# Order of the small steps between two tiles of an input projection: squares, first query copy, rotation

## The reference

```python
h = rms_norm(x, attn_norm)                       # x * rsqrt(mean(x*x) + eps) * g
splits = np.cumsum(IN_SIZES)[:-1].tolist()
q_lat, kv_lat, kr_raw, qb_raw, kb_raw, vb_raw, iq_raw, ik_raw, iw = jnp.split(h @ w_in, splits, axis=-1)
qa = (rms_norm(q_lat, q_a_norm) @ w_q_b).reshape(b, l, N_HEADS_A, NOPE_DIM + ROPE_DIM)
qa_nope, qa_rope = qa[..., :NOPE_DIM], rope(qa[..., NOPE_DIM:], pos)
c_kv = rms_norm(kv_lat, kv_a_norm)
k_rope = rope(kr_raw, pos)
qB = partial_rope(qb_raw.reshape(b, l, N_HEADS_B, HEAD_DIM_B), pos, ROT_DIM_B)
# kB, iq, ik: partial_rope likewise; vB and iw stay as they are
```

## Time and profile before

| what | value |
|---|---|
| median of 3 runs | 4259.19 us (4246.77 to 4260.42) |
| the profiled execution's own time | 4255.5 us |
| its span, first to last instruction | 4253.4 us |
| PE busy | 3778.7 us, 89% |
| DVE, ACT, POOL busy | 52%, 40%, 33% |
| `project`'s loop: first and last `xt_hi` | 15.2 and 535.9 us |

### The profile page before, as it was taken

The page is one execution under the profiler, slowest core; times in us unless marked ns, Lnnn a source line. Parts: engine busy times, 40 slices in busy tenths (PEclk is TensorE's granted clock), DMA queues, the critical chain, the costliest instruction groups (busy, mean ns, idle before and its releaser), DMA issues. The chain is left out here.

```text
span 4253.4 us, 59485 instructions
## 1 busy us (share of the span) xinstructions
PE 3778.7 (89%) x20612; PEld 2900.5 (68%) x20612; DVE 2200.5 (52%) x4236; ACT 1702.1 (40%) x3219; POOL 1386.8 (33%) x890
## 2 busy tenths in 40 slices
PE   7999976877888888888895699899999999999998
PEld 5777743556655555666663577688788778889986
DVE  4222223699988888889953533343044134304421
ACT  3333322556656666666561222232233233223311
POOL 0000000556555565455001000244444444444332
PEclk9999988689989999999996599999999999999999
DMA  4222222110100000000002165334343433433331
GB/s 169 73 80 86 77 65 58 42 34 26 30 22 20 17 20 10 17 16 15 12 6 48 35 229 200 128 89 151 97 118 89 153 114 97 145 106 99 89 109 56
DMA packets 337092, 324.13 MB, mean 76 GB/s; under 512 B 53088, under 2 KB 272832, under 8 KB 336896
## 3 DMA queue, kind: packets, MB, share of 16 engines
q1 hardware_dynamic: 323040, 271.35, 21.9%
q10 hardware_dynamic: 7344, 26.74, 1.5%
q0 software_dynamic: 6528, 23.73, 1.5%
HBM read 251.57 MB, written 71.43 MB: 76 GB/s over the span
## 5 line engine op out<-in xcount | busy, mean ns | idle before, releaser
L2193 DVE TENSOR_SCALAR_CACHE_REDUCE at_hit<-at_score,at_su 128x384 bf16<-128x384 f32 (+13 forms) x406 | 599.6, 1477 | 5.3
L1639 DVE TENSOR_TENSOR ff_a_lo<-ff_prod,ff_a_hi 128x512 f32 (+1 forms) x110 | 410.8, 3735 | 170.7 <-ACT ff_a_hi L1591 170.7
L1494 POOL TENSOR_TENSOR fh_w_lo<-fh_stage,fh_w_hi 128x2048 fp32r<-128x2048 f32 x67 | 309.2, 4615 | 463.4 <-ACT fh_w_hi L1577 463.4
L1925 PE MATMUL at_p_t<-at_ident,at_prob 128*128 128x128 f32 x2176 | 333.6, 290 | 131.8 <-ACT at_prob L2005 130.6
L1494 POOL TENSOR_TENSOR ff_w_lo<-fh_stage,ff_w_hi 128x2048 fp32r<-128x2048 f32 (+1 forms) x68 | 296.3, 4357 | 432.0 <-ACT ff_w_hi L1577 412.8
L1925 PEld LDWEIGHTS at_p_t<-at_ident,at_prob 128*128 128x128 f32 x2176 | 250.7, 145 | 210.9 <-ACT at_prob L2005 177.5
L2005 ACT ACTIVATE at_prob<-at_prob,at_st 128x1024 f32<-128x1024 f32 (+7 forms) x384 | 342.9, 897 | 123.3 <-DVE at_st L2162 123.0
L2020 ACT ACTIVATE at_probt<-at_p_t 128x512 f32<-128x512 f32 (+3 forms) x640 | 313.5, 533 | 163.8 <-PE at_p_t L1925 161.2
L2102 POOL TENSOR_TENSOR at_rel<-at_rel,at_iws 128x512 f32<-128x512 f32 (+3 forms) x304 | 283.7, 933 | 174.7 <-ACT at_rel L2027 174.0
L95 PE MATMUL ff_bank<-fh_h_hi,fh_w_hi 128*128 128x512 f32 (+1 forms) x880 | 309.8, 352 | 10.5 <-DVEq L1626 6.8
L1587 ACT ACTIVATE ff_prod<-ff_bank 128x512 f32<-128x512 f32 (+1 forms) x110 | 57.0, 518 | 646.0 <-PE ff_bank L97 645.8
(11 more groups left out here) (288 smaller groups left out, 8477.9 us busy)
## 6 DMA issues: line engine op xcount, KB each, us to landing
fh_stage<-in_w_gate SPq DMA_DIRECT2D x86, 512.0 KB, 4.0
fh_stage<-in_w_up SPq DMA_DIRECT2D x86, 512.0 KB, 5.2
fh_stage<-in_w_down SPq DMA_DIRECT2D x40, 1024.0 KB, 5.2
pj_xt<-in_xT SPq DMA_DIRECT2D x17, 512.0 KB, 3.6
pj_x<-in_x SPq DMA_DIRECT2D x17, 512.0 KB, 4.4
mx_o<-scr_o SPq DMA_DIRECT2D x17, 512.0 KB, 7.1
mx_x<-in_x SPq DMA_DIRECT2D x17, 512.0 KB, 3.6
scr_x<-mx_x ACTq DMA_DIRECT2D x17, 512.0 KB, 8.2
```

Of the source, the lines that this page charges most:

```text
L1494: pool.tensor_tensor(w_lo[a][:, 0:w], stage[a][:, 0:w], w_hi[a][:, 0:w].bitcast(F32), ALU.subtract).then_inc(s_wlo, 1)
L1639: dve.tensor_tensor(a_lo[:, ds(2 * q + a, 1), to], prod[b][:, 0:gr.Nh].unsqueeze(1), a_hi[:, ds(2 * q + a, 1), to].bitcast(F32), ALU.subtr ...
L1925: mm = pe.transpose(p_t[t_turn.at(n, f) % 2][:, b * P:(b + 1) * P], prob[h % 2][:, a + b * P:a + (b + 1) * P], ident[:, :])
L2193: step(dve.tensor_scalar(h_, s_, cand.bitcast(F32), 0.0, ALU.is_ge, ALU.add, cnt))
```

## The change

ACT: `split` is divided into `cut` (`xt_hi`) and `power` (squares of `x`). In the loop, `power(i + 1)` stands between the copies of z chunks 1 and 2 of tile i; it no longer waits for the four z copies. The copy of QA0 stands ahead of the wait for DVE's inverse means and their root. `cut(i + 1)` follows, then the copies QA1 to T1, and last the root of the next row. DVE: `split` is divided into `cut` (`xt_lo`) and `mean`. `mean(i + 1)` opens the body, with a wait for ACT's root of the row before, since it rewrites that root's input; the rotation stands ahead of `cut(i + 1)`. Nothing changes on PE and SP, nor for the last tile.

```diff
--- before.py
+++ after.py
@@ -238,22 +238,23 @@
             act.sem_inc(s_ev, NB)
             for n in range(6):
                 act.sem_inc(s_qst[n], 16)
-            def split(i):
+            def cut(i):
                 act.wait_ge(s_xt, 16 * i + 16)
                 if not (isinstance(i, int) and i == 0):
                     act.wait_ge(s_zmm, 4 * i)
                 act.activation(xt_hi[:, :, :], xt[:, :, :], ACT.Copy).then_inc(s_hi, 1)
+
+            def power(i):
                 act.wait_ge(s_x, 16 * i + 16)
                 if not (isinstance(i, int) and i == 0):
                     act.wait_ge(s_sq, i)
-                    act.wait_ge(s_zev, 4 * i)
                 act.activation(squares[:, :], x[:, :], ACT.Square, accum_out=stat[:, 0:1]).then_inc(s_sq, 1)
 
             def rstd(i):
                 act.wait_ge(s_inv, i + 1)
                 act.activation(stat[:, 2:3], stat[:, 1:2], ACT.Sqrt).then_inc(s_rstd, 1)
 
-            def take_z(i):
+            def take_z(i, steady=False):
                 act.wait_ge(s_rstd, i + 1)
                 if not (isinstance(i, int) and i == 0):
                     act.wait_ge(s_zr, i)
@@ -262,12 +263,16 @@
                 for c, (a, b) in enumerate(CH):
                     if c == len(CH) - 1 and not (isinstance(i, int) and i == 0):
                         take_fill(i - 1, B_QL)
+                    if c == 2 and steady:
+                        power(i + 1)
                     act.wait_ge(s_zmm, 4 * i + c + 1)
                     act.activation(z[:, a:b], zp[c][:, 0:b - a], ACT.Copy, scale=stat[:, 2:3]).then_inc(s_zev, 1)
                 act.wait_ge(s_zev, 4 * i + 4)
                 act.activation(squares_z[:, 0:QL], z[:, C_Q:C_Q + QL], ACT.Square, accum_out=stat[:, 4:5]).then_inc(s_zsq, 1)
                 act.wait_ge(s_zsq, 2 * i + 1)
                 act.activation(squares_z[:, 0:KVL], z[:, C_KV:C_KV + KVL], ACT.Square, accum_out=stat[:, 5:6]).then_inc(s_zsq, 1)
+                if steady:
+                    take_fill(i - 1, B_QA0)
                 act.wait_ge(s_zinv, i + 1)
                 act.activation(stat[:, 8:10], stat[:, 6:8], ACT.Sqrt).then_inc(s_zrs, 1)
 
@@ -289,28 +294,30 @@
                     act.wait_ge(s_qr, i + 1)
                 act.activation(out, src, ACT.Copy).then_inc(s_ev, 1)
 
-            def post(i):
-                for b in range(B_QA0, NB):
+            def post(i, b0):
+                for b in range(b0, NB):
                     take_fill(i, b)
 
-            split(0)
+            cut(0)
+            power(0)
             for k in range(KD):
                 act.wait_ge(s_wg, k + 1)
                 act.activation(w_hi[:, k, :], stage[k % S][:, :], ACT.Copy).then_inc(s_whi, 1)
             rstd(0)
             take_z(0)
-            split(1)
+            cut(1)
+            power(1)
             rstd(1)
             act.wait_ge(s_wlo, KD)
             with act.Fori(1, LAST) as i:
-                take_z(i)
-                split(i + 1)
+                take_z(i, steady=True)
+                cut(i + 1)
+                post(i - 1, B_QA1)
                 rstd(i + 1)
-                post(i - 1)
             take_z(LAST)
-            post(LAST - 1)
+            post(LAST - 1, B_QA0)
             take_fill(LAST, B_QL)
-            post(LAST)
+            post(LAST, B_QA0)
 
         @block.tensor
         def _(pe):
@@ -385,9 +392,13 @@
             dve.sem_inc(s_qr, 1)
             own = Count(dve, s_vec, 0)
 
-            def split(i):
+            def cut(i):
                 dve.wait_ge(s_hi, i + 1)
                 dve.tensor_tensor(xt_lo[:, :, :], xt[:, :, :], xt_hi[:, :, :].bitcast(F32), ALU.subtract).then_inc(s_lo, 1)
+
+            def mean(i):
+                if not (isinstance(i, int) and i == 0):
+                    dve.wait_ge(s_rstd, i)
                 dve.wait_ge(s_sq, i + 1)
                 own.done(dve.tensor_scalar(stat[:, 3:4], stat[:, 0:1], 1.0 / D, EPS, ALU.mult, ALU.add))
                 dve.reciprocal(stat[:, 1:2], stat[:, 3:4]).then_inc(s_inv, 1)
@@ -446,7 +457,8 @@
                        cos, sin, [tmq[:, a, :, :] for a in range(4)], (s_qr, i + 2))
 
             own.round(0)
-            split(0)
+            cut(0)
+            mean(0)
             dve.wait_ge(s_gain, 16)
 
             def gain(k):
@@ -462,15 +474,18 @@
                 dve.tensor_tensor(w_lo[:, k, :], stage[k % S][:, :], w_hi[:, k, :].bitcast(F32), ALU.subtract).then_inc(s_wlo, 1)
             dve.wait_ge(s_const, 16 * N_CONST)
             z_means(0)
-            split(1)
+            cut(1)
+            mean(1)
             z_rows(0)
             n0, own.per = own.n, own.n + 5
 
             def body(i, last=False):
+                if not last:
+                    mean(i + 1)
                 z_means(i)
+                rotate_qa(i - 1)
                 if not last:
-                    split(i + 1)
-                rotate_qa(i - 1)
+                    cut(i + 1)
                 z_rows(i)
 
             with dve.Fori(1, LAST) as i:
```

## The result

The changed kernel takes 4220.38 us (median of 5 runs, 4217.4 to 4228.85), the one before 4257.01 in the runs beside it: ratio of the means 0.9921, 95% interval 0.9904 to 0.9938, thus 33.6 us less, between 26 and 41 (the medians differ by 36.6). The forecast was 4230, in a range of 4217 to 4247, and a gain of 28.8 us. The profiled execution has a span of 4215.3 us.

The account below looks back on a forecast made before the run. TensorE bounds the kernel, through idle time in each turn's tail and clock dips. 16.8 us (15 turns x 1.12) plus 12.0 (8 dips x 1.50) made 28.8: span 4253.4 to 4224.6, forecast 4230 as median, range 4217 to 4247.

Parts of the forecast that it names:

- The squares cost nothing between the chunks: On ACT, squares needing about 1.14 us fit the 4.89 us idle ahead of the chunk-2 copy, if x has landed.
- c0: PE's first product of the next tile, counted from q (L347 rows' start): from q+9.13 to q+8.01, 16.8 us in 15 turns.
- Rival E: Slower: ACT's new wait for x delays the chunk-2 copy and the copies behind it; time 4272, chance 0.03.
- The 4.3 us more: Slack on ACT after the chunk-2 and QL copies before PE needs QL; x's landing would have to exceed 9.3 us.
- They, and the root behind them, were what PE waited for: Squares and root held ACT 1.79 us ahead of the copies PE needs; moving them brings IQ0 1.82 us earlier.
- the two gaps: On the way to c0: rotation to low half on DVE, taken as 0.28 us; low half to c0, 0.15.
- The dips: PE's clock at 1.2 GHz after the tail's idle in 8 of 15 turns; all gone, 8 x 1.50 = 12.0 us.
- Rivals B and C: PE's dips stay: B, once in two turns, time 4242, chance 0.13; C, in every turn, time 4253, chance 0.04.
- Rival D: Another wait holds QB0's copy on ACT, so IQ0 stays near q+7; time 4259, chance 0.04.
- The swap: DVE rotates before making the low half; worth about nothing alone, perhaps slightly against, c0 near q+7.9 without it.
- QA0 ahead of the root: On ACT, QA0's copy takes the 0.61 us hole before L272; it fits, as two copies took 0.87.

Follow-up runs that it names:

- e1: Changed kernel with the squares back in the tail, behind the high half and ahead of QA1's copy; ratio to the kernel before 0.9962.
- e6: Only the change's first part (squares, mean, root moved); QA0 next to QA1 behind the high half, low half ahead of the rotation; ratio to the kernel before 0.9933.
- e4: Kernel before with DVE's new order alone (mean, rotation, low half), ACT as before; ratio to the kernel before 1.0007.
- e7: Changed kernel with two useless 128x1024 copies on ACT between the copies of QA1 and QB0; one execution, 4247.85 us.
- e5: Changed kernel with the next input's low half made by POOL in the loop, DVE only rotating and writing rows; ratio to the kernel before 0.9985.
- e10: Changed kernel with the low half on POOL and ACT writing the queries' unrotated part straight from PSUM, without DVE's copy; ratio to the kernel before 0.9956.
- e8: Changed kernel with one useless 128x1024 copy on ACT between the copies of QA1 and QB0; one execution, 4215.79 us.
- e3: Changed kernel with DVE's old order, low half ahead of the rotation; ratio to the kernel before 0.9921.
- e2: Changed kernel with QA0's copy back behind the high half, next to QA1; ratio to the kernel before 0.9925.

## Why the prediction was right

- *The squares cost nothing between the chunks:* shown by the idle time behind them, 1.04 us in the turn above and never under 0.64. The forecast had 0.6 there. It let DVE's row copy start at c0+0.13 and x be issued at c0+10.9; the row copy starts at c0-0.32 (238.97), before the low half has ended, and x is issued at c0+10.46. Rival E didn't come about, as no load was late enough to hold chunk 2. The 4.3 us more that it reckoned before PE would stall stay an estimate: no run has a later load.
- *They, and the root behind them, were what PE waited for:* IQ0 was forecast at q+5.15 and came at q+5.23; e1 gives the squares' share, e6 shows that this part alone is enough, and the root's share, 0.75 us, is read from rows. The 0.08 by which IQ0 is later lies in QB0's copy, which starts at q+4.59 where the last turn has q+4.51, both times behind a copy of QA1 at q+4.07; why isn't shown.
- *c0:* forecast q+7.68 to q+8.10, taken as 8.01, measured 7.85. Of the two gaps the first was 0.04 and not 0.28: the wait of the earlier trace rows stands ahead of `z_rows`, which has three waits of its own, and doesn't go over to a neighbour with one (that this is the reason is argued, not shown). The second was 0.24, not 0.15. So this term was 15 x 1.25 = 18.8 us in place of 16.8. The idle time in front of c0 was to be 0.5 to 0.8 us and is 0.36 in PE's row: c0 is 0.61 later than the q+7.24 that T0 alone would allow, but T0's rows are drawn until q+7.49.
- *The dips:* forecast 12.0 us back, measured 8 x (33.15 - 31.63) = 12.2. Rivals B and C fall: both short gaps are there and the granted clock is 1.00 over all 15 turns. The Trainium skill's rule that the prediction cited against itself ("TensorE: Matmul & The Clock Gate", section "A second HAM failure mode: psum-queue depth-cycling") tells of a clock that swings because of short idle times; this trace doesn't bear it out for the 0.33 and 0.36 us left here. What the kernels with dips have in common:

  | kernel | longest idle time, us | idle times of the tail, sum | c0 at full clock | dipped turns of 15 |
  |---|---|---|---|---|
  | e4 | 1.97 | 2.52 | q+9.65 | 8 |
  | before | 2.07 | 2.26 | q+9.13 | 8 |
  | e7 | 2.22 | 2.22 | q+8.89 | 6 |
  | e5 | 1.57 | 1.90 | q+8.77 | 4 |
  | e1 | 0.93 | 1.57 | q+8.68 | 0 |
  | e10 | 1.23 | 1.56 | q+8.43 | 0 |
  | e8 | 1.13 | 1.13 | q+7.85 | 0 |
  | changed | 0.36 | 0.69 | q+7.85 | 0 |

  My theory in e7 was the length of the wait in one piece. All waits with dips are longer than all without, but the count doesn't follow it: 2.22 us gave fewer dips than 1.97. It does follow the sum of the tail's idle times, and the place of c0. No run separates these, so which of them counts stays open. One reading of the prediction was loose: its two windows in the earlier trace rows start at q+8.33 and q+7.11, not at the same place; at q+8.33 the short turn (250.52 to 253.82) is granted 1.00 as well, so nothing hangs on it.
- *Rival D* fell: IQ0 moved by 1.74 us, so nothing else held QB0's copy near its old place.
- *The swap:* said to be worth about nothing or slightly against; it is against, by 0.25 us a turn (e3). The remark had the size a little low: it put c0 near q+7.9 without the swap, and it is at q+7.63.
- *QA0 ahead of the root:* my step counted it as fitting its hole, which it does; it buys nothing (e2).

Sum by measured terms: 18.8 + 12.2 = 31.0 us, where the forecast had 28.8. The time's 33.6 agrees with 31 within its interval; the rest of the span's 38.1 lies in stages that the change doesn't touch. The terms were low by 2.0 and 0.2 us. Luck had a part in the second: that all dips would go came true, but what keeps them away isn't shown.

## What to carry to other kernels

Ask of each instruction in front of a copy that frees a PSUM bank whether TensorE waits for it; what belongs to the next tile can go where its engine waits for products anyway, even if it then waits for a load there, as long as some of that idle time is left behind it. The turn without the next tile's work, at a loop's end, is a free model of the loop with that work moved. And price an idle time twice: with waits of 2.07 and 0.19 us cut to 0.33 and 0.36, the turn at full clock got 1.25 us shorter, and the dips that went with them had cost 0.8 us a turn more on the mean.

## What was not expected of the hardware

In two places GpSimd held up VectorE in full, not by a share, and as far as rows show it was not slowed itself: its subtraction took 2.36 us, and `at_qb_lo`, of the same shape and on the same engine in the kernel before, 2.36 on the mean. While GpSimd subtracted two 128x1024 tensors for 2.36 us, VectorE's 128x512 copy took 1.95 us instead of 0.43 (e5) and, with that copy gone, a 128x128 product 1.83 instead of 0.28 (e10); they ended 0.29 and 0.15 us after GpSimd did. The Trainium skill, "Advanced Engine Details and Errata", section "GPSIMD Details", says that the two share a read and a write interface and conflict when VectorE runs in a two-port mode or has two inputs in SBUF. The trace agrees for the product, which has two inputs there; the copy has one, and no row shows its mode. In both cases GpSimd had started first and VectorE's instruction ended only behind it, in all 15 turns; the other order of the two was not run.
